# A hybrid decode step: ranks instead of compares in the router, the rows of two experts picked from SBUF, and another order of weight loads

## What is computed

```python
def hier_moe(h, w_rg, b_rg, w_re, b_re, w_gate, w_up, w_down):
    t = h.reshape(bsz * L, D)
    glog = (t @ w_rg).astype(f32)
    gprob = jax.nn.softmax(glog, axis=-1)
    gsel = jnp.argmax(glog + b_rg.astype(f32), axis=-1)          # one of 4 groups
    gw = jnp.take_along_axis(gprob, gsel[:, None], axis=-1)
    elog = (t @ w_re).astype(f32).reshape(-1, N_EGROUPS, EXPERTS_PER_GROUP)
    elog = jnp.take_along_axis(elog, gsel[:, None, None], axis=1)[:, 0]
    eprob = jax.nn.softmax(elog, axis=-1)
    _, topi = lax.top_k(elog + b_re.astype(f32)[gsel], TOP_K)    # 2 of its 4 experts
    ew = jnp.take_along_axis(eprob, topi, axis=-1)
    ew = ew / jnp.sum(ew, axis=-1, keepdims=True)
    ...
    return jnp.einsum('nef,efd->nd', silu(hg) * hu * gates, w_down)

x = x + mix
x = x + hier_moe(rmsnorm(x, norm_ffn_w), ...)
gate = sigmoid(rmsnorm(x, norm_ple_w) @ w_ple_gate)
x = x + gate * (p @ w_ple_proj)
y = rmsnorm(x, final_norm_w)
```

## Time and profile before

| | us |
|---|---|
| median of 3 runs (lowest, highest) | 643.93 (643.51, 645.4) |
| the profiled execution, its own time | 642.05 |
| span of its trace | 640.3 |
| PE busy / DVE / ACT / POOL | 597.1 / 291.5 / 175.1 / 80.1 |
| bytes moved by DMA | 179.67 MB, 281 GB/s over the span |

### The profile page before, as it was taken

The page is one execution under the profiler, slowest core; times in us unless marked ns, Lnnn a source line. Parts: engine busy times, 40 slices in busy tenths (PEclk is TensorE's granted clock), DMA queues, the critical chain, the costliest instruction groups (busy, mean ns, idle before and its releaser), DMA issues.

```text
span 640.3 us, 9666 instructions
## 1 busy us (share of the span) xinstructions
PE 597.1 (93%) x3812; PEld 395.6 (62%) x3812; DVE 291.5 (46%) x944; ACT 175.1 (27%) x421; POOL 80.1 (13%) x101
## 2 busy tenths in 40 slices
PE   6999999989998999999999799999988897899996
PEld 5888888878486887788786433333333332344684
DVE  3596288668469899454211731101100001116574
ACT  3223238511642433636101411111110100100343
POOL 1400023320001212210000011211110201100000
...
GB/s 295 253 200 174 39 197 255 358 344 229 134 100 99 242 242 183 260 109 304 369 394 354 220 416 414 426 424 430 425 426 423 430 427 422 425 414 303 2 1 68
DMA packets 45863, 179.67 MB, mean 281 GB/s; under 512 B 3963, under 2 KB 12863, under 8 KB 37360
## 3 DMA queue, kind: packets, MB, share of 16 engines
...
...
## 4 chain that ended last, share of the span: by engine, by line
PE 73%; DMA 19%; DVE 3%; ACT 2%; issue 1%; SPq 1%; DVEq 0%; ACTq 0%
PE bank L936 24%; DMA arena<-in_w_exp_up 15%; PE bank L1416 11%; PE bank L1209 9%; PE bank L1454 6%; PE bank L1552 4%; DMA arena<-in_w_in 4%; PE bank L955 1%; DVE arena L1881 1%; PE bank L967 1%; PE bank L1427 1%; PE bank L1052 1%; PE bank L1273 1%; PE bank L1167 1%; PE bank L1113 1%
## 5 line engine op out<-in xcount | busy, mean ns | idle before, releaser
L936 PE MATMUL bank<-hT,arena 128*128 128x264 f32 x768 | 178.6, 393 | 2.6 <-DMA arena<-in_w_in 2.6
L936 PEld LDWEIGHTS bank<-hT,arena 128*128 128x128 f32 x768 | 146.7, 193 | 29.6 <-issue 4.7
L1416 PE MATMUL bank<-arena,hT 128*64 128x512 f32 x512 | 120.8, 627 | 16.6 <-DMA arena<-in_w_exp_up 11.4
L1416 PEld LDWEIGHTS bank<-arena,hT 128*64 128x64 f32 x512 | 39.4, 144 | 89.3 <-issue 87.6
L1889 DVE SCALAR_TENSOR_TENSOR hT<-hT,sq,bank 128x256 f32<-128x256 f32 x16 | 7.7, 480 | 135.5 <-ACT hT L1804 135.5
L1881 DVE TENSOR_TENSOR arena<-arena 128x256 f32<-128x256 f32 (+7 forms) x146 | 60.4, 458 | 17.4 <-ACT arena L1696 10.9
L1454 PE MATMUL bank<-arena,sq 128*64 128x512 f32 x256 | 58.5, 598 | 0.9 <-ACT sq L1809 0.9
L1209 PE MATMUL bank<-arena 128*128 128x264 f32 x256 | 58.1, 387 | 0.9 <-issue 0.9
L1209 PEld LDWEIGHTS bank<-arena 128*128 128x128 f32 x256 | 48.3, 190 | 10.0 <-issue 2.0
L1626 ACT ACTIVATE arena<-bank 128x264 f32<-128x264 f32 x40 | 15.6, 391 | 110.0 <-PE bank L936 110.0
L1804 ACT ACTIVATE hT<-bank 128x256 f32<-128x256 f32 x16 | 6.1, 384 | 139.9 <-PE bank L1416 139.9
...
## 6 DMA issues: line engine op xcount, KB each, us to landing
...
arena<-in_w_in SPq DMA_DIRECT2D x12, 2048.0 KB, 11.2
...
```

The source lines that it names most:

```text
L936: last = mm(ps[:, 0:T], w[:, k, j * P:(j + 1) * P], hT[:, k], start=(k == 0), stop=(k == KT - 1))
L1416: last = mm(bank[p][r, :].rearrange("p (w f) -> p w f", w=2), xgT[:, p, k % 4, CAP * (k // 4):CAP * (k // 4) + CAP], gu[:, :, k, FF // 2 * ...
```

## The change

1. **Router.** The square sums go straight to token order: token_sums multiplies squares by a column of ones on PE, ACT takes the root of 128x2 and 8x1 values, DVE the reciprocal. Router parts 4 and 5 move ahead of mix 7. The masks come from ranks: all pairs inside each quad of biased logits are subtracted and compared (128 x 240 elements, with a tie offset), the sum over the rivals is the rank, and rank under 0.5 or 1.5 gives best and chosen.
2. **Rows of experts 0 and 1.** pick_rows multiplies a float32 one-hot by htok on PE (six 64x512 matmuls); DVE copies the result to xg. Expert 1's stands behind gate_up(0). POOL gathers from expert 2 on, by row numbers of a smaller "idx".
3. **PE.** The table of experts 0 to 3 moves between the halves of gate_up(0). The filler keep_busy shrinks from three 512-column matmuls to two of 256.
4. **SP.** load_down(2) no longer waits; the PLE inputs go behind expert 3 and wait for the second pick (they overwrite htok). The order of down weights is DOWN_AFTER; down 15 stands behind the pair rows.
5. **The branch** moves from turn 12 to 10 (CHECK).
6. **The end.** The last norm uses token_sums too.

The diff, cut to its core:

```diff
-CHECK = 12
+CHECK = 10
 PLE_JOBS = 10
 WARM = 5
+DOWN_AFTER = {6: [7], 7: [8], 8: [9], 9: [], 10: [10], 11: [11], 12: [], 13: [12], 14: [13, 14], 15: [15]}
...
         mt_ready, oh_ready, tab_ready = sem("mt_ready"), sem("oh_ready"), sem("tab_ready")
-        xg_clear = sem("xg_clear")
+        pick_ready, rows_ready = sem("pick_ready"), sem("rows_ready")
+        second_picked, second_in = sem("second_picked"), sem("second_in")
         pair_in, acc_ready = sem("pair_in"), sem("acc_ready")
         main, over = PackedSems(sem, "m"), ExpertSems(sem, "o")
...
@@ -626,10 +634,7 @@
             load_down(3)
             eng.wait_ge(v_full, jv["mix", KT - 1] + 1)
             load_gate(2)
-            eng.wait_ge(hrow_out, 48)
-            eng.wait_ge(main.rows[0], 16)
             load_down(2)
-            ple_weights(ld_pp)
 
             def load_pairs():
                 eng.wait_ge(main.gu_full, SENT + 1)
@@ -667,10 +672,13 @@
                     return
                 if t == E - 1:
                     load_pairs()
-                if t + 1 < E and t + 1 != CHECK:
-                    next_down(t + 1)
+                for d in DOWN_AFTER[t]:
+                    next_down(d)
 
             next_expert(SLOTS)
+            eng.wait_ge(hrow_out, 48)
+            eng.wait_ge(second_picked, 1)
+            ple_weights(ld_pp)
...
-            next_down(CHECK)
...
+                        eng.wait_ge(tab_ready, 1)
                     if 3 <= t < SENT + 3:
                         scatter_halves(t - 3)
 
-            eng.wait_ge(xg_clear, 2)
             eng.wait_ge(hrow_out, 48)
-            eng.wait_ge(v_took, jv["idx"] + 1)
-            gather_halves(0)
-            eng.wait_ge(tab_ready, 1)
-            move_tokens(1, CHECK + 3)
+            eng.wait_ge(rows_ready, 1)
+            move_tokens(2, CHECK + 3)
...
+            def norm_sum(x):
+
+                ps = open_a("norm", 2)
+                eng.wait_ge(sq_sum, SQ_BASE[3])
+                mm(ps[:, 0:T], ones, x, start=True, stop=True).then_inc(a_full, 1)
+
+            def token_sums(ps, x, start):
+
+                for i, (t0, n) in enumerate(TOK):
+                    last = mm(ps[0:n, i:i + 1], x[:, t0:t0 + n], ones[:, 0:1], start=start and i == 0,
+                              stop=not start and i == 2, skip_group_check=True)
+                return last
...
-                if c >= 6:
-                    for k in ((0, 1, 2, 3) if c == 6 else (4, 5)):
+                if c == 6:
+                    for k in range(6):
                         router_part(k)
-            for c in range(6, KT):
-                router_part(c)
-            norm_sum(1, sq[:, 0])
+            router_part(6)
+            ps = open_a("norm", 1)
+            eng.wait_ge(sq_sum, SQ_BASE[2])
+            token_sums(ps, sq[:, 0], True)
+            router_part(7)
+            eng.wait_ge(sq_done, 2 * KT)
+            token_sums(ps, sq[:, KT - 1], False).then_inc(a_full, 1)
...
-                    mm(ps[:, :], ident, K[:, 0:512], start=True, stop=True)
+                    mm(ps[:, 0:2 * P], ident, K[:, 0:2 * P], start=True, stop=True)
...
+            def pick_rows(ps, hot):
+
+                for i, (t0, n) in enumerate(TOK):
+                    eng.wait_ge(a_took, ja["ht", i, 1] + 1)
+                    for c, r in enumerate(halves):
+                        last = mm(ps[r, :], hot[0:n, i], htok[0:n, i, HALF * c:HALF * c + HALF], start=(i == 0), stop=(i == 2))
+                return last
+
+            ps = open_a("pick")
+            eng.wait_ge(pick_ready, 1)
+            pick_rows(ps, first_hot).then_inc(a_full, 1)
             ps = open_v("idx")
-            eng.wait_ge(oh_ready, 1)
-            for i in range(3):
-                for c in range(3):
+            eng.wait_ge(oh_ready, TAB0 - 2)
+            for t in range(2, TAB0):
+                for i in range(3):
                     for r in halves:
-                        last = mm(ps[r, 0:1], OH[:, 0, i], places[:, i, c:c + 1], start=(i == 0 and c == 0),
-                                  stop=(i == 2 and c == 2))
+                        last = mm(ps[r, 3 * (t - 2):3 * (t - 1)], OH[:, t, i], places[:, i, 0:3], start=(i == 0), stop=(i == 2))
...
+                eng.wait_ge(rv_ready, 1)
                 for t in range(first, turns):
-                    eng.wait_ge(oh_ready, t + 1)
+                    eng.wait_ge(oh_ready, max(t + 1, TAB0))
...
-            keep_busy(bank[4 + jv["tab", 0] % 4], 3)
-            eng.wait_ge(rv_ready, 1)
-            table(0, 0, TAB0)
+            keep_busy(bank[4 + jv["tab", 0] % 4], 1)
...
                     if t == 0 and k == 3:
                         last.then_inc(gu_half, 1)
+                        table(0, 0, TAB0)
...
-                eng.wait_ge(main.rows[p], t // 2 * 16 + 16)
+                if t >= 2:
+                    eng.wait_ge(main.rows[p], t // 2 * 16)
+                elif t:
+                    eng.wait_ge(second_in, 1)
+                else:
+                    eng.wait_ge(a_took, ja["pick"] + 1)
...
-            eng.wait_ge(a_took, ja["ht", 2, 1] + 1)
             halves_rows(0)
+            keep_busy(bank[4 + jv["tab", 0] % 4], 1)
             def turns(first, stop):
                 for t in range(first, stop):
                     halves_gate_up(t)
                     if t == 0:
+                        eng.wait_ge(pick_ready, 2)
+                        eng.wait_ge(v_took, jv["idx"] + 1)
+                        pick_rows(bank[6], second_hot).then_inc(second_picked, 1)
                         table(1, TAB0, E)
...
-            eng.wait_ge(ple_took, PLE_JOBS)
+            eng.wait_ge(ple_took, CHECK - 1)
...
-            out_row(open_v("out", 1, 0), 1, 0)
+            out_row(open_v("out", 1, 0), 1, 0).then_inc(v_full, 1)
             out_row(open_a("out", 2, 0), 2, 0)
-            norm_sum(3, sq_end[:, 0], 2)
-            ps = open_v("sd")
-            eng.wait_ge(a_took, ja["norm", 3] + 1)
-            turn_factors(ps, 0).then_inc(v_full, 2)
+            ps = open_a("norm", 3)
+            eng.wait_ge(sq_sum, 3 * KT - 5)
+            token_sums(ps, sq_end[:, 0], True)
+            eng.wait_ge(sq_done, 4 * KT)
+            token_sums(ps, sq_end[:, KT - 1], False).then_inc(a_full, 2)
             out_row(open_a("out", 0, 1), 0, 1).then_inc(a_full, 2)
...
-                if c:
+                if 1 <= c <= 5:
                     weighted(c - 1, "mix", R_FFN)
-                if c >= 2:
+                if 2 <= c <= 5:
                     add_square(c - 1)
-            weighted(KT - 1, "mix", R_FFN)
-            add_square(KT - 1)
+                if c >= 5:
+                    weighted(c, "mix", R_FFN)
+                if 5 <= c < KT - 1:
+                    add_square(c)
...
-            pair(top(r1[:, 0], lg, ALU.max), tt(biased, ex, rbe, ALU.add))
...
-            tt(Mt[:, 0:2].rearrange("p t (g e) -> p t g e", g=EG), first[:, 0:2], second[:, 0:2], ALU.add).then_inc(mt_ready, 1)
-            tt(Mt[0:NS, 2].rearrange("p (g e) -> p g e", g=EG), first[0:NS, 2], second[0:NS, 2], ALU.add).then_inc(mt_ready, 1)
+            link(tt(by_token(biased), rt[:, :, :], rb.rearrange("p (o e) -> p o e", o=1).to_broadcast([P, 3, 20]), ALU.add))
+            link(tt(ahead, quads(biased, False), quads(biased, True), ALU.subtract))
+            link(tt(beats, ahead, tie.rearrange("p (o i) j -> p o i j", o=1).to_broadcast([P, 15, 4, 4]), ALU.is_gt))
+            link(nc.vector.tensor_reduce(rank.rearrange("p (q e) -> p q e", e=4), beats, AX.X, ALU.add))
+            pair(ts(best, rank, 0.5, ALU.is_lt), ts(chosen, rank, 1.5, ALU.is_lt))
+            tt(Mt[:, 0:2].rearrange("p t (g e) -> p t g e", g=EG), chosen16[:, 0:2], ohb[:, 0:2]).then_inc(mt_ready, 1)
+            tt(Mt[0:NS, 2].rearrange("p (g e) -> p g e", g=EG), chosen16[0:NS, 2], ohb[0:NS, 2]).then_inc(mt_ready, 1)
+            pair(top(r1[:, 0], lg, ALU.max), tt(g4, ex, ohb))
...
-            one_hots(0, 1)
+            tt(first_hot, K[:, K_IOTA:K_IOTA + CAP].rearrange("p (o s) -> p o s", o=1).to_broadcast([P, 3, CAP]),
+               slot1[:, :, 0:1].to_broadcast([P, 3, CAP]), ALU.is_equal).then_inc(pick_ready, 1)
             nc.vector.tensor_reduce(most[:, :], ps[:, 3 * E:4 * E], AX.X, ALU.max).then_inc(v_took, 1)
             took("cnt")
-            one_hots(1, TAB0)
-            ts(first_at[:, :], full("idx")[:, 0:1], AWAY, ALU.add, K[:, K_HALF:K_HALF + 1], ALU.add).then_inc(v_took, 1)
...
+            one_hots(2, TAB0)
+            one_hots(0, 2)
+            tt(second_hot, K[:, K_IOTA:K_IOTA + CAP].rearrange("p (o s) -> p o s", o=1).to_broadcast([P, 3, CAP]),
+               slot1[:, :, 1:2].to_broadcast([P, 3, CAP]), ALU.is_equal).then_inc(pick_ready, 1)
+            tt(rs[:, 0], lg, bc(r1[:, 0]), ALU.subtract).then_inc(r_in, 1)
...
+            eng.wait_ge(a_full, ja["pick"] + 1)
+            nc.vector.tensor_copy(xg[:, 0], bank[ja["pick"] % 4][:, :]).then_inc(a_took, 1)
```

(10 more changed lines are left out.)

150 lines of the change are left out of this document (62 added, 88 removed).

## The result

| | before | after |
|---|---|---|
| median of 4 runs beside each other (lowest, highest), us | 643.80 (643.51, 645.4) | 636.65 (634.83, 638.2) |
| the profiled execution, us | 642.05 | 634.83 |
| span of its trace, us | 640.3 | 633.0 |
| PE / DVE / ACT / POOL busy, us | 597.1 / 291.5 / 175.1 / 80.1 | 598.1 / 291.2 / 174.9 / 76.8 |

The ratio after to before is 0.9883, 95% interval 0.9848 to 0.9918: 7.15 us faster by the medians, where 11.05 were forecast. The time lies inside the range of the prediction, 3.75 above its middle.

What follows compares the result with a forecast made beforehand. Weight loads bound the middle, PE the tail; at the front both are short. From 642.05, less 10.0 at add_pairs and 1.05 in the last norm, came 631.0, or 632.9 on the median's scale; range 629.5 to 638.0.

Steps and rivals of the forecast that it cites:

- Router and picked rows: Front: Mt 2.05 us earlier, rows picked on PE, expert 0 starting at 363.6 against 368.00, 4.4 earlier.
- Expert 1: Front: of expert 0's 4.4 us only 1.0 is left at expert 1's start, taken as 1.2.
- rival A: Front: clock falls anyway on first pick, transposes and expert 0; 4.3 us passed to the whole stream, 637.2; chance 0.18.
- Loads at the front: Before gate 4: 8 us of loads moved away gain nothing, idle instead; the stream moves 1.2 with expert 1.
- Late downs: Experts 14 and 15: up 14 has two fewer loads ahead, landing at 548.7; up 15 lands at 568.8.
- PE and stream meet: Expert 15: PE is ready at 569.0, its weights land at 568.8.
- Rival E: Late downs: order brings nothing since gates wait for slots; only 1.2 + 1.05 stay, 641.7; chance 0.05.
- From expert 10 to 15 PE has no slack: After the branch, inside rival B: if the branch costs twice its 4.11 us, all of it shows.
- Rival B: Branch at ten: costs twice its 4.11 us while PE has no slack, 637.0; chance 0.10.
- Rival D: After the branch: PE stays at 1.2 GHz, slower than before; two whole turns give 656.5; chance 0.04.
- What follows is unchanged: After the pair adds: add_pairs starts 10.0 us earlier, the work behind stays as before, PLE matmuls at 590.8.
- Rival C: End: pair adds hide, stream slightly faster; floor is PLE gate weights landing at 589.3, giving 631.4 or 630; chance 0.08.

Runs made afterwards that it cites:

- late_downs_only: The kernel before with only the new order of late down weight loads added; 638.51 us, ratio 0.9876.
- expert_four_halves: The changed kernel with gate and up of expert 4 loaded in halves, the first once PE is halfway through expert 1; 634.3 us, ratio 0.9847.
- no_branch: The changed kernel without the overflow branch on all five engines, overflow path left out; median 634.8 us, ratio 0.9796.
- after_again: The changed kernel run once more, nothing changed; 637.4 us, ratio 0.9889.
- fill_pairs_wait: The changed kernel with seven more 256-column matmuls between expert 15 and the transposes of the pair sums; 634.85 us, ratio 0.9838.

## Why the prediction was right or wrong

Counted from the router's transposes, which stood at 353.24 in the trace it was made from, its steps against after:

| step | forecast | after |
|---|---|---|
| expert 0 | 10.4 | 9.62 |
| expert 1 | 23.3 | 22.51 |
| expert 9 | 127.7 | 128.05 |
| expert 10 | 149.7 | 149.72 |
| expert 14 | 197.2 | 196.70 |
| expert 15 | 215.8 | 216.31 |
| adds of the pairs | 220.8 | 222.36 |
| PLE matmuls | 237.6 | 243.07 |
| from there to the end | 38.46 | 38.81 |

**Router and picked rows: right in kind, too small.** What the change does ahead of the transposes cancels, as was assumed (56.54 from the output projection's matmuls against 56.71 in before). The 240-element step cost 0.44, not 0.54. The copy of the picked rows stood at 358.56 since the pick on PE was the last there and not DVE's nine small instructions; the table's wait on rv had its cover (rv at 362.39, the first half ended at 364.4). Expert 0 came 5.1 earlier than in before, not 4.4.

**Expert 1: right that little is left.** It started 1.8 earlier than in before, and 1.2 of low clock on it took most of that back. This is rival A's mechanism in part: not on the first pick and expert 0, which ran at 2.94 and 7.28, but on expert 1. Between 354 and 374 PE had only gaps of 0.28, 0.79, 0.25 and 0.26, and the clock fell at about 372.7 (0.83 in 372 to 373, then 0.50) while it was busy with small matmuls; of the ten profiles with this code up to expert 1 that have no filler, nine show 8.15 to 8.75 us for it and one 7.09. The prediction had read from the trace of before that only a longer single idle does this. The Trainium skill (TensorE: Matmul & The Clock Gate, section A second HAM failure mode: psum-queue depth-cycling) says that frequent micro-idles between groups of matmuls can make the clock swing. The trace agrees in that no long idle came before the fall, but it cost 1.2 and not 4.3, and whether the short gaps were its cause no run shows. Measured against late_downs_only, whose expert 0 had low clock, the front is worth more: expert 2 comes 2.1 earlier in after, against 0.6 from before's profile.

**Loads at the front: nearly.** DMA idled for 2.4 us ahead of gate 4, where 3 had been named. Down 2 at its new place costs 0.5 to 0.9, not 0. What the prediction overlooked is that this idle time itself could be used: expert_four_halves gained 2.65 from it.

**Late downs: right.** The weights of experts 14 and 15 came as counted, within 0.6 (up 14 landed at 547.0, up 15 at 567.3). PE waited 0.93 for up 15, 0.16 to 1.43 in the other profiles with this order: "PE and stream meet" held, though a wait for up 15 was also named as a sign of being wrong. Rival E is refuted.

**Branch: right in the sum, with half of the account.** Experts 10 and 14 came within 0.5 of the count in after (in after_again expert 10 was 1.7 later than that). "From expert 10 to 15 PE has no slack" nearly held for time added to PE: it had the 0.93 that it waited for up 15. It says nothing of time taken away, since the stream is as late as PE: no_branch gives PE 4.6 us at expert 10, and it loses them to waits at experts 12 and 14 and the low clock behind the first. Rival B did not come (the idle was 4.08); what 4.11 more would have cost was not run, and the 0.93 could have covered only a part. Rival D did not come either: after 9.52 on expert 10 the next experts took 7.09.

**The end: here it failed.** The step was "What follows is unchanged". Adding the pairs no longer follows on expert 15 at once. PE waits for DVE's adds (the prediction itself had PE ready at 576.0 and the adds at 577.5), and that wait takes the clock: 3.69 us on the pair sums and down 15, which fill_pairs_wait gave back. Next, the pair rows: the adds started 6.05 after expert 15 (573.48 against 567.43), not 5.0 (574.0 less 569.0), and expert 15 was 0.55 late, 1.6 together; with the rest of 0.2 that is the 5.5 by which the PLE matmuls missed. The forecast had a rival with low clock at the front and one behind the branch, none at the wait that it had counted itself. Rival C's floor, the landing of the PLE gate weights, was not reached: the last landed at 588.7, 5.5 ahead of the PLE matmuls.

**Tail.** 0.70 instead of 1.05 (39.51 to 38.81).

The ledger, in the two profiles: 5.5 at the PLE matmuls and 0.35 in the tail, less 2.12 by which the transposes stood earlier, nearly all of it for reasons ahead of the change, is 3.75, the miss. From the transposes on the change gave 5.2 us, less than half of the 11.05 forecast. The range held because it reached up to rival A, and by luck: with the transposes where before's profile had them the sum is 636.65 + 2.12 = 638.8, outside 638.0. A's 637.2 is near the time, but its mechanism made up only 1.2 of it. That the medians differ by more (7.15, and 6.6 for after_again) than the 5.2 of the steps is not explained; before's one profile may have had a good front, as late_downs_only, with the same code up to there, was 1.45 later at expert 2.
